# Another order of the first transfers, and a query projection done one token tile at a time

## The reference, cut to what matters

```python
def first_block(x, positions, norm_mix_g, w_in, ...):
    cos, sin = rope_tables(positions, x.dtype)
    h = rmsnorm(x, norm_mix_g[l])          # x: 1 x 256 x 1024
    proj = h @ w_in[l]                     # w_in: 1024 x 2048
    p, q, k, v = jnp.split(proj, [512, 1024, 1536], axis=-1)
    q = apply_rope(q.reshape(b, s, 4, 2, 64), cos, sin)
    k = apply_rope(k.reshape(b, s, 4, 2, 64), cos, sin)
    ...
```

## Time and profile before

| | |
|---|---|
| runs | 1049.94, 1051.09, 1052.87 us, median 1051.09 |
| profiled execution: span from first to last instruction | 1048.3 us |
| PE busy | 1025.7 us, 98% |
| PE weight loads busy | 866.8 us, 83% |
| VectorE busy | 842.9 us, 80% |
| ScalarE busy | 665.9 us, 64% |
| mean granted TensorE clock | 0.998 |
| transfers | 253.62 MB, mean 242 GB/s |

### The profile page before, as it was taken

How to read it: one execution, slowest core, us unless ns; L and a number is a source line. 1 busy time by engine, 2 the same in 40 slices (tenths; PEclk the granted TensorE clock), 3 DMA queues, 4 the chain that set the end, 5 groups by cost and what they waited for, 6 DMA issues and landing times. The chain is left out here.

```text
span 1048.3 us, 14957 instructions
## 1 busy us (share of the span) xinstructions
PE 1025.7 (98%) x5574; PEld 866.8 (83%) x5574; DVE 842.9 (80%) x1091; ACT 665.9 (64%) x834; POOL 33.2 (3%) x40
## 2 busy tenths in 40 slices
PE   7999999999999999999999999999999999999997
PEld 6778999999999888989879777777878777878784
DVE  5856776766777777787868799999999999999977
ACT  5554755555565755565544677777777777777764
POOL 1001000000000100100210000000000000000000
PEclk9999999999999999999999999999999999999999
DMA  9734456474624445333214889898989898989881
GB/s 346 264 121 141 140 182 224 143 236 146 217 86 161 161 162 166 121 122 122 81 33 167 323 318 376 353 383 348 385 349 386 349 385 346 381 353 386 346 328 44
DMA packets 82711, 253.62 MB, mean 242 GB/s; under 512 B 4160, under 2 KB 42176, under 8 KB 62656
## 3 DMA queue, kind: packets, MB, share of 16 engines
q1 hardware_dynamic: 82624, 252.50, 64.4%
HBM read 251.44 MB, written 1.05 MB: 241 GB/s over the span
## 5 line engine op out<-in xcount | busy, mean ns | idle before, releaser
L1064 DVE TENSOR_TENSOR WL<-raw,WH 128x2048 fp32r<-128x2048 f32 x230 | 493.7, 2176 | 92.1 <-ACT WH L544 92.0
L544 ACT ACTIVATE WH<-raw 128x2048 fp32r<-128x2048 f32 x231 | 419.6, 1823 | 126.3 <-PE bank L2000 80.5
L1998 PE MATMUL bank<-WH,MXH 128*128 128x512 f32 x552 | 226.3, 410 | 0.2 <-DVE WL L1064 0.2
L2000 PE MATMUL bank<-WH,MXL 128*128 128x512 f32 x552 | 215.2, 390 | 0.0
L1999 PE MATMUL bank<-WL,MXH 128*128 128x512 f32 x552 | 215.0, 390 | 0.0
L1998 PE MATMUL bank<-HTH,WH 128*128 128x256 f32 x576 | 165.3, 287 | 2.4 <-DVE HTL L1087 1.2
L1999 PE MATMUL bank<-HTL,WH 128*128 128x256 f32 x576 | 162.9, 283 | 0.0
L2000 PE MATMUL bank<-HTH,WL 128*128 128x256 f32 x576 | 162.9, 283 | 0.0
L1998 PE MATMUL bank<-WH,HTH 128*128 128x512 f32 x348 | 140.2, 403 | 1.4 <-DVE WL L1111 1.0
L1999 PE MATMUL bank<-WL,HTH 128*128 128x512 f32 x348 | 135.7, 390 | 0.0
L1998 PEld LDWEIGHTS bank<-WH,MXH 128*128 128x128 f32 x552 | 103.7, 188 | 27.2 <-issue 7.0
(11 more groups left out here) (396 smaller groups left out, 1105.0 us busy)
## 6 DMA issues: line engine op xcount, KB each, us to landing
raw<-in_exp_w_up SPq DMA_DIRECT2D x52, 1024.0 KB, 8.1
raw<-in_exp_w_gate SPq DMA_DIRECT2D x52, 1024.0 KB, 8.3
raw<-in_exp_w_down SPq DMA_DIRECT2D x52, 1024.0 KB, 6.8
raw<-in_w_in SPq DMA_DIRECT2D x34, 1024.0 KB, 5.3
raw<-in_w_up SPq DMA_DIRECT2D x22, 1024.0 KB, 5.3
raw<-in_w_down SPq DMA_DIRECT2D x11, 1024.0 KB, 5.1
raw<-in_w_out SPq DMA_DIRECT2D x8, 1024.0 KB, 5.0
raw<-in_w_o SPq DMA_DIRECT2D x4, 1024.0 KB, 5.7
```

The lines of the kernel that those rows point to most:

```text
L544: e.activation(WH[i % HL][:, 0:n], raw[i % RAW][:, 0:n], ACT.Copy).then_inc(a_wh, 1)
L1064: e.tensor_tensor(l, r, h.bitcast(F32), ALU.subtract).then_inc(v_wl, 1)
L1998: e.matmul(out_, ah, bh, start=start, stop=False)
L2000: return e.matmul(out_, al, bh, start=False, stop=stop)
```

## The change

The query projection is written out: token tile 0 first, in four quarters (two pieces, two halves of each), each quarter with its own waits; tile 1 of x is turned between the third and the fourth quarter; then token tile 1 with both pieces. The columns lie in banks 0 to 3 and are copied per tile (128 tokens) instead of for both tiles together (256 tokens), so there are sixteen copies on each of ScalarE and VectorE instead of eight. The two query pieces are loaded in halves with a semaphore for the first half of each, and tile 1 of x is loaded behind them. There are eight filler products instead of nine. Some semaphores of later loads are merged into shared counts.

```diff
 SyncE
-            for t in range(T):
-                e.dma_start(X[:, t, :], a["x"][t * P:(t + 1) * P, :]).then_inc(d_x[t], 16)
+            e.dma_start(X[:, 0, :], a["x"][0:P, :]).then_inc(d_x[0], 16)
             e.dma_start(pt[:, :], a["pt"]).then_inc(d_pt, 16)
-            load_pieces(0, 2)
+            for i in range(2):
+                src = piece_src(a, PIECES[i])
+                dst = raw[i][:, :].rearrange("p (k n) -> p k n", k=4)
+                e.dma_start(dst[:, 0:2, :], src[:, 0:2, :]).then_inc(d_first[i], 16)
+                e.dma_start(dst[:, 2:4, :], src[:, 2:4, :]).then_inc(d_raw[i], 16)
+            e.dma_start(X[:, 1, :], a["x"][P:2 * P, :]).then_inc(d_x[1], 16)
 ...
-            e.dma_start(pool_a, a["pool_a"]).then_inc(d_pa, 16)
-            e.dma_start(pool_w, a["pool_w"].rearrange("g c d -> c g d")).then_inc(d_pw, 16)
+            e.dma_start(pool_a, a["pool_a"]).then_inc(d_pool, 16)
+            e.dma_start(pool_w, a["pool_w"].rearrange("g c d -> c g d")).then_inc(d_pool, 16)
 ScalarE (VectorE the same, with the low parts)
+        def mix_at(t, k):
+            return bank[k // 2][:, (k % 2) * 256 + t * 128:(k % 2) * 256 + (t + 1) * 128]
-            columns("mix", "norm_mix_g", 0, (4, 5, 6, 7), HTH, (0, 1))
-            e.wait_ge(d_raw[0], 16)
-            e.activation(WH[0][:, 0:PC // 2], raw[0][:, 0:PC // 2], ACT.Copy).then_inc(a_w0, 1)
-            e.activation(WH[0][:, PC // 2:PC], raw[0][:, PC // 2:PC], ACT.Copy).then_inc(a_wh, 1)
-            columns("mix", "norm_mix_g", 0, (4, 5, 6, 7), HTH, (2, 3))
-            split(1)
+            def mix_columns(t, k0, k1):
+                for k in range(k0, k1):
+                    if k % 2 == 0:
+                        e.wait_ge(p_cols, COL["mix", 4 * t + k // 2])
+                    e.activation(HTH[:, k, t * 128:(t + 1) * 128], mix_at(t, k), ACT.Copy,
+                                 scale=ptcol("norm_mix_g", k)).then_inc(a_colh, 1)
+            def first_half(i):
+                e.wait_ge(d_first[i], 16)
+                e.activation(WH[i][:, 0:PC // 2], raw[i][:, 0:PC // 2], ACT.Copy).then_inc(a_w0, 1)
+            def second_half(i):
+                e.wait_ge(d_raw[i], 16)
+                e.activation(WH[i][:, PC // 2:PC], raw[i][:, PC // 2:PC], ACT.Copy).then_inc(a_wh, 1)
+            mix_columns(0, 0, 4)
+            first_half(0)
+            mix_columns(0, 4, 6)
+            second_half(0)
+            mix_columns(0, 6, 8)
+            first_half(1)
+            second_half(1)
+            mix_columns(1, 0, 8)
             e.wait_ge(d_x[1], 16)
             squares("mix", 1, X[:, 1, :], ss[:, 1:2])
             split(2)
 TensorE
-            columns(X, (4, 5, 6, 7), ((d_x[0], 16), (d_x[1], 16)))
-            warm(9, 0)
+            def turn_mix(t):
+                e.wait_ge(d_x[t], 16)
+                for k in range(8):
+                    m = e.transpose(mix_at(t, k), X[:, t, k * 128:(k + 1) * 128], ident)
+                    if k % 2:
+                        m.then_inc(p_cols, 1)
+            def first_q(kh, c):
+                wh, wl = (v[kh][:, :].rearrange("p (k n) -> p k n", k=4) for v in (WH, WL))
+                ks = (2 * c, 2 * c + 1)
+                e.wait_ge(v_coll, COL["mix", 2 * kh + c])
+                e.wait_ge(a_wh if c else a_w0, kh + 1)
+                for part in (HTH, HTL):
+                    for k in ks:
+                        e.matmul(bank[4][:, :], part[:, 4 * kh + k, 0:128], wh[:, k, :],
+                                 start=(part is HTH and kh == 0 and k == 0), stop=False)
+                e.wait_ge(v_wl if c else v_w0, kh + 1)
+                for k in ks:
+                    m = e.matmul(bank[4][:, :], HTH[:, 4 * kh + k, 0:128], wl[:, k, :], start=False,
+                                 stop=(kh == 1 and k == 3))
+                return m
+            def second_q(kh):
+                wh, wl = piece(kh, 4)
+                for k in range(4):
+                    if k % 2 == 0:
+                        e.wait_ge(v_coll, COL["mix", 4 + 2 * kh + k // 2])
+                    m = three(bank[5][:, :], HTH[:, 4 * kh + k, 128:256], HTL[:, 4 * kh + k, 128:256], wh[:, k, :],
+                              wl[:, k, :], kh == 0 and k == 0, kh == 1 and k == 3)
+                m.then_inc(p_used, 1)
+            turn_mix(0)
+            warm(8, 7)
+            first_q(0, 0)
+            first_q(0, 1)
+            first_q(1, 0)
+            turn_mix(1)
+            first_q(1, 1).then_inc(p_tok0, 1)
+            second_q(0)
+            second_q(1)
 ...
-            for c, n in enumerate("qk"):
-                for kh in range(2):
-                    tok_half(HTH, HTL, PI[n, kh], kh, (4 + 2 * c, 5 + 2 * c), tok0=kh, cols=None if c else "mix",
-                             ready=None if c or kh else [(v_w0, 1), (v_w0, 1), (v_wl, 1), (v_wl, 1)])
+            for kh in range(2):
+                tok_half(HTH, HTL, PI["k", kh], kh, (6, 7), tok0=kh)
 ...
-            e.wait_ge(d_pa, 16)
+            e.wait_ge(d_pool, 32)
 ...
-            e.wait_ge(d_pw, 16)
```

More of the change, by code:

```diff
@@ L112 @@
 COL = numbered([(s, j) for s in ("mix", "attn", "ffn", "n1", "ssd0", "ssd1", "ml0", "ml1")
-                for j in range(4 if s in ("mix", "ffn", "n1") else 2)])
+                for j in range(8 if s == "mix" else 4 if s in ("ffn", "n1") else 2)])
 P_CUM = numbered(["sums", "turned", "max"])
@@ L413, in build @@
         d_x = [sem(f"d_x{t}") for t in range(T)]
-        d_cn, d_cn2, d_pt, d_pos, d_br, d_pa, d_pw, d_gb, d_wsm, d_iota, d_wrt, d_gbf, d_out = (
-            sem("d_" + n) for n in ("cn", "cn2", "pt", "pos", "br", "pa", "pw", "gb", "wsm", "iota", "wrt", "gbf",
+        d_cn, d_cn2, d_pt, d_pos, d_br, d_pool, d_gains, d_small, d_iota, d_out = (
+            sem("d_" + n) for n in ("cn", "cn2", "pt", "pos", "br", "pool", "gains", "small", "iota",
                                     "out"))
@@ L449, in build @@
         a_w0, v_w0 = sem("a_w0"), sem("v_w0")
+        d_first = [sem(f"d_first{i}") for i in range(2)]
+        def mix_at(t, k):
+            return bank[k // 2][:, (k % 2) * 256 + t * 128:(k % 2) * 256 + (t + 1) * 128]
         def sync(e):
@@ L474, in sync @@
             load_pieces(5, 7)
-            e.dma_start(pool_a, a["pool_a"]).then_inc(d_pa, 16)
-            e.dma_start(pool_w, a["pool_w"].rearrange("g c d -> c g d")).then_inc(d_pw, 16)
+            e.dma_start(pool_a, a["pool_a"]).then_inc(d_pool, 16)
+            e.dma_start(pool_w, a["pool_w"].rearrange("g c d -> c g d")).then_inc(d_pool, 16)
             load_pieces(7, 18)
             e.wait_ge(p_pmix, 4)
-            e.dma_start(gb, a["norm_final_g"].partition_broadcast(P)).then_inc(d_gb, 16)
+            e.dma_start(gb, a["norm_final_g"].partition_broadcast(P)).then_inc(d_gains, 16)
             load_pieces(18, 51)
-            e.dma_start(ws_raw, a["wsm"]).then_inc(d_wsm, 16)
+            e.dma_start(ws_raw, a["wsm"]).then_inc(d_small, 16)
             load_pieces(51, PI["mk", 1])
             e.wait_ge(p_cb, 2)
-            e.dma_start(wr_raw, a["wrt"]).then_inc(d_wrt, 16)
+            e.dma_start(wr_raw, a["wrt"]).then_inc(d_small, 16)
             load_pieces(PI["mk", 1], NP)
@@ L487, in sync @@
             e.dma_start(iota, a["iota"].partition_broadcast(P)).then_inc(d_iota, 16)
-            e.dma_start(gbf, a["norm_f_w_2"].partition_broadcast(P)).then_inc(d_gbf, 16)
+            e.dma_start(gbf, a["norm_f_w_2"].partition_broadcast(P)).then_inc(d_gains, 16)
             ex = {}
@@ L767, in scalar @@
                 if c == 3:
-                    e.wait_ge(d_wsm, 16)
+                    e.wait_ge(d_small, 16)
                     e.activation(wsh[:, 0:256], ws_raw, ACT.Copy).then_inc(a_whs, 1)
@@ L1108, in vector, with mix_columns, first_half, second_half @@
             e.wait_ge(d_pt, 16)
[L1109 to L1117, removed]
+            def mix_columns(t, k0, k1):
+                for k in range(k0, k1):
+                    ts = slice(t * 128, (t + 1) * 128)
+                    if k % 2 == 0:
+                        e.wait_ge(a_colh, 2 * COL["mix", 4 * t + k // 2])
+                    m = e.scalar_tensor_tensor(out=HTL[:, k, ts], in0=mix_at(t, k), scalar=ptcol("norm_mix_g", k),
+                                               in1=HTH[:, k, ts].bitcast(F32), op0=ALU.mult, op1=ALU.subtract)
+                    if k % 2:
+                        m.then_inc(v_coll, 1)
+            def first_half(i):
+                e.wait_ge(a_w0, i + 1)
+                e.tensor_tensor(WL[i][:, 0:PC // 2], raw[i][:, 0:PC // 2], WH[i][:, 0:PC // 2].bitcast(F32),
+                                ALU.subtract).then_inc(v_w0, 1)
+            def second_half(i):
+                e.wait_ge(a_wh, i + 1)
+                e.tensor_tensor(WL[i][:, PC // 2:PC], raw[i][:, PC // 2:PC], WH[i][:, PC // 2:PC].bitcast(F32),
+                                ALU.subtract).then_inc(v_wl, 1)
+            mix_columns(0, 0, 4)
+            first_half(0)
```

(12 more changed lines are left out.)

## The result

Over 20 runs each, the changed kernel takes 1052.59 us (1051.06 to 1053.46) and the kernel before 1050.91 us (1049.66 to 1052.87): ratio 1.0016, 95% interval 1.0010 to 1.0022, or 1.7 us (1.1 to 2.3) more. The forecast was 1.2 us more.

What follows compares the result with a forecast made beforehand. VectorE's line was taken to bound the kernel between 29 and 43 us: the 3.1 us lead turns into a hole, and a 1.2 us later key split carries through, 1051.09 + 1.2 = 1052.3 us, range 1049.0 to 1055.5.

Steps and rivals of the forecast that it cites:

- What decides: Between 29 and 43 us VectorE sets the end; 8.55 us from first key split's end to second key piece unchanged.
- signs of being wrong: Split before 20.5; no second-key hole; rows behind 44 us not 1.2 us later; clock leaving 1.00 before the tail.
- Transfers: First loads: parameter table lands at 6.0, query halves at 7.4, 8.7, 10.0, 11.4, x tile 1 at 12.7 us.
- Start of the projection: TensorE starts the query projection at 9.4 instead of 12.51 us, a lead of 3.1 us.
- TensorE's end of the query: TensorE ends tile 0's fourth quarter at 16.7 and token tile 1 at 22.2 us.
- rival 2: Clock falls in the hole at the second key piece, 1.2 + 5.1 us, so 1057.4; chance 0.07.
- Small copies: Sixteen small column copies instead of eight on ScalarE and VectorE, 0.27 us each for 128x128.
- Key split: VectorE's split of the first key piece ends at 21.7 us instead of 20.47, 1.2 us later.
- Hole and end: TensorE stands 2.6 us before the second key piece, starts it at 30.2; 1.2 us carries to the end.
- Two bounds: Time change from -0.2 us (columns at 0.18) to +2.8 us (columns at 0.37 to 0.39, first half 0.3 later).
- Rival 1: Lead at the query start kept in whole or part, 1051.09 - 3.1 = 1048.0 us; chance 0.10.
- Rivals 3 and 4: 3: halves not in turn, first lands late, 1054.9, chance 0.05; 4: cheaper copies, nothing moves, 1051.1, chance 0.06.

Runs made afterwards that it cites:

- experiment 1: VectorE's table of angles moved to its very start, in the changed kernel (1048.82 us) and in the kernel before (1049.20 us).
- e1: Changed kernel with the table of angles computed at VectorE's very start, positions loaded early: 1048.82 us, ratio 0.9981 to the kernel before.
- e2: Kernel before with the table of angles computed at VectorE's very start, positions loaded early: 1049.20 us, ratio 0.9991.
- e5 again: Second execution of the changed kernel with the two query pieces loaded whole instead of in halves: 1054.96 us.
- e9: Changed kernel with the parameter table loaded behind the two halves of the first query piece instead of ahead of them: 1053.38 us.
- the control: Changed kernel run again unaltered, on another chip: 1052.71 us, ratio 1.0023 to the kernel before.
- e5: Changed kernel with the two query pieces loaded whole instead of in halves, first execution: 1055.79 us.
- e6: Changed kernel with x tile 1 loaded right behind tile 0, weights still in halves: 1053.48 us, ratio 1.0030.
- e3: Changed kernel with seven identity products on TensorE between the first and second key piece: 1052.39 us, ratio 1.0023.
- e4: Changed kernel with ScalarE's squares of x tile 1 behind its first key piece copy, VectorE's means behind its own: 1051.80 us, ratio 1.0013.
- e8: e1 with ScalarE's squares behind the split of the first key piece and 8 filler records instead of 16: 1048.49 us, ratio 0.9982.

## Why the prediction was right, point by point

**What decides** (VectorE's line, not TensorE's share of 98%): right, shown by experiment 1 and the table. Of the signs of being wrong two came all the same: the rows behind 44 us stand 2.2 us later and not 1.2, and the clock left 1.00 ahead of the tail. Both are sizes, answered below. The 8.55 us from the end of the key split to the second key piece, said to be left alone, are 31.04 - 22.49 = 8.55.

**Transfers**: the mis-sized term. The first half and x tile 1 landed about 1.0 us later than worked out. The rate of 1.33 us per half holds between neighbours (8.4, 9.8, 11.1, 12.4, 13.7); the offset in front does not. The new order has two further issues on SP, not three as I wrote; the timeline has them at 0.43 to 0.48 us each. The Trainium skill (DMA: Bandwidth & Descriptors, Anatomy of one DMA — SWDGE (gpsimd) path) has a fit with about 2 us of fixed cost per transfer, measured on another path than these. These landings, 1.3 us apart, show that no such cost is paid in series here.

**Start of the projection**: 9.70 against a forecast 9.4, within its bound; it waited 0.20 us for the half that came late.

**TensorE's end of the query**: forecast, the last product of tile 1 ends at 22.2; it starts at 22.21. That is luck, two errors that cancel. The half came 1.0 us late, and the turning of tile 1, taken at 1.72 us, took 0.80 (14.73 to 15.53). I had its step from the first transposes, which are slower: in the lines above, eight transposes take 1.73 us from 4.84 to the next instruction at 6.57 (0.213 us a step), and 0.80 from 14.73 to 15.53 (0.109, less what the next product overlaps). The early step is twice the later one, as in the stretch where the clock reads 0.50 (0.427 against 0.227). So the 1.00 of the clock column in the first microseconds, which I held against rival 2, can't be taken as a reading; the steps say the lower level, until about 8.6 us in the changed kernel and 10.5 in the kernel before.

**Small copies**: eight took 2.18 us on ScalarE and 2.16 on VectorE, 0.26 each less overlap; I had 0.27.

**Key split**: forecast to end at 21.7, ended at 22.49. The late landing passed into the third low half (ready at 14.11, forecast 13.1) and the turning of tile 1 (14.73, forecast 13.65); 0.2 us came back since ScalarE could start 0.42 us behind the first transpose (I had taken 0.65, with two transposes at the early step); from there on each step was as forecast.

**Hole and end**: forecast 2.6 us and 30.2; measured 2.76 and 31.04. The shift at 43 us was forecast 1.2; it was 2.2 in the trace and 1.7 (1.1 to 2.3) in the runs. Of the trace's 2.2 us, 1.2 are the forecast, 0.8 the key split that ended late (22.49 against 21.7) and 0.2 the clock's fall. Two bounds were added up wrongly. With columns at 0.18 us and x tile 1 at 12.7 the split would end some 0.4 us earlier than before, not 0.2, if VectorE's part were free. And my bounds with the spread of the runs give 1049.8 to 1055.7 where I wrote 1049.0 to 1055.5. The measured time lies inside either.

**Rival 1** had a wrong price. I gave the whole lead as 3.1 us, the difference of the first products. It was 2.8 at the first product (9.70 against 12.51). But the turning of tile 1 (0.8 us), which stood ahead of the query before, now stands within it, and so does 1.0 us of short waits, mostly for VectorE's low halves; the last query product starts at 22.21 instead of 23.25. The lead at the end of the query is 1.0 us, and e1 against e2 shows 0.9. So the whole lead, 1048.0, was not to be had from this change by itself.

**Rival 2** half happened. The clock fell behind this hole in the changed kernel, in e5 again and in e9, and not in the control, in e5 and in e6, with holes of 2.7 to 2.8 us each. But it cost 0.2 us at the first scores and not 5.1: I had kept the second key piece at the lower clock to its end, where the clock was back after eight to nine products (1.7 us lost), and had let only 0.39 us of slack absorb it; the last rope gives more. The Trainium skill (TensorE: Matmul & The Clock Gate, HAM oscillation — how this bites in real kernels) warns of waits between bursts of products. It named the right danger, and three of the six traces with this hole agree.

**Rivals 3 and 4**: the halves came in turn, and the split did not stay.

## What to carry to other kernels

A start that is made earlier on the bound engine pays only up to the next place where that engine already waits, even for 0.1 us: look for such waits first, and follow the engine that causes them back to its own start. Price a lead at the end of the reordered block, not at its first instruction, since work moved into the block comes off it. Work that needs only small early inputs (here a table of angles, 4.1 us) belongs in the idle time before the first weights land; that alone took 1.3 us off the first scores of the old kernel and 4.4 off those of the changed one.

A step read at a kernel's start is not the step of the same instruction later: the transposes here took twice as long in the first microseconds as at 14.7 us. Take prices from rows of the same stretch.

## What the runs showed of the hardware that I had not expected

- A hole of 2.7 to 2.8 us in TensorE's work, after steady work, was followed by a fall of the granted clock to 1.2 GHz in three of six executions, and in none of three when there was a filler or a hole of 2.1 us or less (e3, e4, the kernel before). In the changed kernel the fall came 1.4 us after the work had begun again. A shorter hole is not safe by this: in e5_whole_pieces the clock fell at 11.2 us, behind a wait of 2.2.
- TensorE's first instructions ran at half pace although the clock column reads 1.00: transposes at 0.213 us a step (0.109 later), and in e8 products at 0.427 (0.227 later) up to 14.0 us.
- The landing of the first transfers differs by up to 1.9 us between executions of the same order (first half of the first piece at 7.7 and 9.6 in e1 and e8), while neighbours behind it keep their distance of 1.3 us.
